# Output projections after two mixers: a weight tile's split is moved ahead, and one pair of output tiles goes k tile by k tile

## The chip, the core and the metric

The kernel runs on one core of a Trainium2 chip. The metric is the time of one execution on the device, in microseconds (us). Engines are named as in the profile: PE is TensorE (PEld its weight loads), DVE is VectorE, ACT is ScalarE, POOL is GpSimd, SP is SyncE, which here issues every DMA.

## What is computed

Two blocks of two layers each run one after the other. Each layer is a mixer and a convolutional FFN with residual sums and norms. Two mixers matter here, the "first" and the "second" one:

```python
def _even_mixer(h, w_in, w_out, lb, norm_g, sinks, cos, sin):      # first block, layer 0: the first mixer
    z = h @ w_in
    ...
    oa = _hgrn2(...)                       # 4 heads of 128
    oa = oa * rsqrt(mean(oa * oa) + eps) * norm_g
    oa = oa * silu(ag)
    ob = _swa(q, k, v, sinks)              # window attention, 8 heads of 64
    return jnp.concatenate([oa, ob], axis=-1) @ w_out          # "out1"

# second block, layer 0: the second mixer (even_mix), on 256 context and 512 latent tokens
#   fourier_mix: 4 groups of 128 columns;  gated linear attention: 4 heads of 128
#   each head: o * rsqrt(mean(o * o) + eps) * g_gla_out * silu(gate)
#   concatenate([fourier, gla]) @ w_even_out                   # "out2"
```

The modulation of every layer is `silu(c) @ w + b`, from the conditioning vectors c (three rows of 1024 in all). For the layers behind the first one these products are made on DVE during the FFNs.

## The kernel before, in words

**Layout.** Activations are kept transposed: a tile is 128 features by all tokens (512 latent tokens, or 768 with the 256 context tokens, which come as segments of 256 and 512 columns). A product is made at higher precision out of two fp32r parts: the activations lie in `h_hi` and `h_lo`, a weight tile in `w_hi` and `w_lo`, and each k tile (128 of the 1024 input features) takes three matmuls, hi by hi, lo by hi, and hi by lo, per segment. With 512 tokens an output tile is 8 k tiles x 3 = 24 matmuls, with 768 tokens it is 48.

**Weights.** All weight tiles of the program have one running number g. Tile g uses buffer g % 2 of `w_raw`, `w_hi`, `w_lo` and PSUM banks 2(g % 2) and 2(g % 2) + 1. Four steps belong to each tile, each on another engine and in that engine's own program order: `sp_fetch(g)` (L257, after `w_lo` of g - 2), `act_split(g)` (L267: ACT copies `w_raw` into `w_hi`, after the load and after the product of g - 2), `dve_split(g)` (L277: `w_lo` = `w_raw` - `w_hi`), `pe_product(g)` (L286). `pe_product` waits for `w_lo` of its tile and can wait for each k tile of the activations before its matmuls. `pe_pair` (L306) makes two output tiles together: k tile c of the first, then k tile c - 3 of the second. It is used at present for the first two tiles of the input projections and of the FFNs.

**Output projections.** `pe_residual`, `act_residual` and `dve_residual` (L1108 to L1150) run eight output tiles: tiles 22 to 29 for out1, 175 to 182 for out2. ACT's and DVE's loops split tile base + n + 1 at the head of step n, so the first tile (22, 175) is split at the end of the stage before and the second (23, 176) is the first thing of these loops. For out1, PE makes behind its second tile a small product, the "guess" of the mean (L1070), which waits for the first residual sum (`dve_add`, L340).

**Around out1.** ACT's order is: `act_window` (its last work is the four copies into `h_hi`, L944), `act_vectors` (L430: it waits for the DMA of all conditioning vectors into `c_act`, issued by SP in `sp_vectors` when the window attention's last product is done, and then applies SiLU to 128 x 3072), `act_tables` (a table load, L252), then `act_residual`. DVE's order is `dve_window` (ends with the four `h_lo`, L971), five small coefficient operations (L1214 to L1219), `dve_residual`. SP's is `sp_vectors`, three loads of `m_raw`, then `sp_tiles`, the first of which is tile 25's fetch, waiting for `w_lo` of tile 23.

**Around out2.** The last part of the second mixer, `pe_gla`, `act_gla` and `dve_gla`, goes head by head, 0 to 3, with PSUM banks 4 and 5 or 6 and 7: PE mixes (L1834 to L1836), ACT copies out and squares (L1873, L1879), PE sums the squares (L1840), ACT takes the root (L1884, L1887), DVE scales and gates (L1947, L1949), ACT makes `h_hi` (L500) and DVE `h_lo` (L506) of k tile 4 + h. k tiles 0 to 3 come from the Fourier part and are there long before. Then PE's `pe_out2` waits for `h_lo` of k tile 7, the last head's, ahead of its first matmul:

```python
def pe_out2(k):
    pe_residual(k, BASE["out2"], TALL, k.h_hi, k.h_lo, [("h_lo", ("gla", KD - 1))], ("rms", 1))
```

Of the kernel before, what the change touches and what calls it, by code (L numbers as in the profile page):

```python
# [17 lines left out]
KD = D // P  # L18
CTX, LAT = 256, 512
TALL = CTX + LAT  # L20
# [1084 lines left out]
        sp_fetch(k, base + i + 3)  # L1105


def pe_residual(k, base, tokens, hi, lo, ready, st):  # L1108

    for n in range(KD):  # L1110
        pe_product(k, base + n, tokens, hi, lo, ready if n == 0 else ())
        if n == 1 and st[0] == "ln":
            pe_guess(k, st, base)
    pe_sums(k, st)


def act_residual(k, base, st, split=None):

    for n in range(KD):
        act_split(k, base + n + 1)  # L1120
        if n == 2:
            if st[0] == "ln":
                act_guess(k, st)
            act_square(k, st, 0, base)
        if n >= 2:
            act_square(k, st, n - 1, base)
    if split is not None and st[0] == "ln":
        act_split(k, split)
    act_square(k, st, KD - 1, base)
    if split is not None and st[0] == "rms":  # L1130
        act_split(k, split)


def dve_residual(k, base, tokens, gates, st, slots=None, x_ready=None):
    for n in range(KD + 1):
        if n == 1 and x_ready:
            k.nc.vector.wait_ge(*k.seen(*x_ready))
        if n:
            dve_add(k, base + n - 1, n - 1, tokens, gates(n - 1))
        if n <= 2:  # L1140
            dve_split(k, base + n + 1)
        for f in (0, 1) if n == 2 else (n - 1,) if n > 2 else ():
            dve_center(k, st, f, base)
            dve_sum_x(k, st, f)
        if 2 < n < KD:
            dve_split(k, base + n + 1)
        for f in (0, 1) if n == 2 else (n - 1,) if n > 2 else ():
            dve_sum_squares(k, st, f)
        for j in slots[n] if slots and n < KD else ():
            dve_job(k, FFN_JOBS, j)  # L1150
# [692 lines left out]
def act_gla(k):  # L1843
    act = k.nc.scalar
    q, kk, (e0, e1), comb, _, turned, state = gl_views(k)
    v3 = lambda a: a.rearrange("p (n c) -> p n c", c=CHUNK)
    s16 = 1.0 / 16.0
    act_gl_gates(k, 0)
    for i in range(len(GL_STEPS)):
        act_decay(k, "g", i, gl_combs(k)[i % 3], s16)  # L1850
        if i == 2:
            act_gl_gates(k, 1)
    act.activation(k.gb_flat(4, 4), k.gb_flat(4, 4), ACT.Silu).then_inc(*k.tick("gl_silu"))
    act_tables(k)
    act.wait_ge(*k.seen("kd_arg", "g"))
    act.activation(comb, comb, ACT.Exp, scale=s16).then_inc(*k.tick("kd_decay", ("g", 0)))
    for d in range(2):
        for b in range(0, 12, 8):
            n = min(8, 12 - b)
            act.wait_ge(*k.seen("turn", ("gkd", d, b)))  # L1860
            got = k.ps[:, 4 + b // 4:6 + b // 4, :].rearrange("p b (i t) -> p (b i) t", t=P)[:, 0:n, :]
            act.activation(k.gkdt[d][:, b:b + n, :], got, ACT.Copy).then_inc(*k.tick("turned_out", ("gkd", d, b)))
        if d == 0:
            act.activation(comb, e1, ACT.Exp, scale=s16).then_inc(*k.tick("kd_decay", ("g", 1)))
    act.activation(e0, e0, ACT.Exp, scale=s16).then_inc(*k.tick("q_decay", ("g", 0)))
    act.wait_ge(*k.seen("q_arg"))
    act.activation(e1, e1, ACT.Exp, scale=s16).then_inc(*k.tick("q_decay", ("g", 1)))
    act.activation(k.gends[:, :, :], k.gends[:, :, :], ACT.Exp, scale=s16).then_inc(*k.tick("end_decay", "g"))
    for h in range(4):
        o, b0 = comb[:, (h % 2) * TALL:(h % 2 + 1) * TALL], 4 + 2 * (h % 2)  # L1870
        act.wait_ge(*k.seen("mixed", ("g", h)))
        for t0, tn, bank in segments(TALL):
            last = act.activation(o[:, t0:t0 + tn], k.ps[:, b0 + bank, 0:tn], ACT.Copy)  # L1873
        last.then_inc(*k.tick("mixed_out", ("g", h)))
        act.wait_ge(*k.seen("mixed_out", ("g", h)))
        for i, (t0, tn, bank) in enumerate(segments(TALL)):
            if h:
                act.wait_ge(*k.seen("summed", ("g", h - 1, i)))
            act.activation(k.tmp[i][:, 0:tn], o[:, t0:t0 + tn], ACT.Square).then_inc(*k.tick("squared", ("g", h, i)))  # L1879
        act.wait_ge(*k.seen("summed", ("g", h, 1)))  # L1880
        if h:
            act.wait_ge(*k.seen("normed", ("g", h - 1)))
        for t0, tn, bank in segments(TALL):
            last = act.activation(k.rstd[:, t0:t0 + tn], k.ps[:, b0 + bank, 0:tn], ACT.Ln, scale=1.0 / P, bias=k.col("eps6"))  # L1884
        last.then_inc(*k.tick("root_log", ("g", h)))
        act.wait_ge(*k.seen("root_log", ("g", h)))
        act.activation(k.rstd[:, :], k.rstd[:, :], ACT.Exp, scale=-0.5).then_inc(*k.tick("root", ("g", h)))  # L1887
        act_high(k, "gla", 4 + h, slice(0, TALL), o)


def dve_gla(k):
# [42 lines left out]
    for n in range(NC2 - 1):  # L1934
        for d in range(2):
# [6 lines left out]
                                                k.gends[:, d, f * NC2 + c:f * NC2 + c + 1], k.ps[:, bank, f * P:(f + 1) * P], ALU.mult, ALU.add)  # L1942
            last.then_inc(*k.tick("state", ("g", d, n + 1)))
    for h in range(4):
        o = comb[:, (h % 2) * TALL:(h % 2 + 1) * TALL]
        dve.wait_ge(*k.seen("root", ("g", h)))
        dve.scalar_tensor_tensor(o, o, k.col("ggla", h), k.rstd[:, :], ALU.mult, ALU.mult).then_inc(*k.tick("normed", ("g", h)))  # L1947
        dve.wait_ge(*k.seen("normed", ("g", h)))
        dve.tensor_tensor(o, o, k.z2[:, 4 + h, :], ALU.mult).then_inc(*k.tick("value", ("gla", 4 + h)))  # L1949
        dve_low(k, "gla", 4 + h, slice(0, TALL), o)  # L1950


def pe_out2(k):
    pe_residual(k, BASE["out2"], TALL, k.h_hi, k.h_lo, [("h_lo", ("gla", KD - 1))], ("rms", 1))

# [299 lines left out]
def act_program(k):  # L2257
    act_start(k)
    act_in1(k)
    act_hgrn(k)  # L2260
    act_window(k)
    act_vectors(k)
    act_tables(k)
    act_residual(k, BASE["out1"], ("ln", 0), BASE["up", 0, 0, 0] + 1)
    act_norm(k, 0, split=BASE["up", 0, 0, 0] + 1)
    act_ffn(k, 0, 0, LAT, ("ln", 1))
    act_norm(k, 1, plain=k.ph)
    act_residual(k, BASE["pool"], ("ln", 2), BASE["up", 0, 1, 0] + 1)
    act_norm(k, 2, split=BASE["up", 0, 1, 0] + 1)
    act_ffn(k, 0, 1, LAT, ("ln", 3), None, act_context)  # L2270
    act_norm(k, 3)
    act_rms(k, 0, LAT, BASE["in2"] + 1)
    act_in2(k)
    act_fourier(k)
    act_gla(k)
    act_residual(k, BASE["out2"], ("rms", 1), BASE["up", 1, 0, 0] + 1)
    act_rms(k, 1, TALL, BASE["up", 1, 0, 0] + 1)
    act_ffn(k, 1, 0, TALL, ("rms", 2), BASE["qkv"] + 1)
    act_rms(k, 2, TALL, BASE["qkv"] + 1)
    act_attention(k)  # L2280
    act_residual(k, BASE["attout"], ("rms", 3), BASE["up", 1, 1, 0] + 1)
    act_rms(k, 3, LAT, BASE["up", 1, 1, 0] + 1)
    act_ffn(k, 1, 1, LAT, ("rms", 4))
    act_final(k)


def dve_program(k):
    dve_start(k)
    dve_in1(k)
    dve_hgrn(k)  # L2290
    dve_window(k)
    dve_out1(k)
    dve_norm(k, 0, split=BASE["up", 0, 0, 0] + 1)
    k.nc.vector.wait_ge(*k.seen("c_act", "all"))
    dve_ffn(k, 0, 0, LAT, gates1(k, 0, 5), ("x_scaled", (0, KD - 1)), ("ln", 1), lambda: dve_coefficients1(k, 1, 0, 1, (0, 1, NMOD - 1)))
    dve_norm(k, 1, behind=lambda f: dve_pool_window(k, f))
    dve_pool(k)
    dve_norm(k, 2, split=BASE["up", 0, 1, 0] + 1)
    dve_ffn(k, 0, 1, LAT, gates1(k, 1, 5), ("x_scaled", (2, KD - 1)), ("ln", 3), lambda: dve_coefficients2(k, 0, 0, 0, "gmix", (1,)), dve_context)
    dve_norm(k, 3)  # L2300
    dve_rms(k, 0, LAT, BASE["in2"] + 1)
    dve_in2(k)
    dve_fourier(k)
    dve_gla(k)
    dve_coefficients2(k, 1, 0, 3, "gffn")
    dve_residual(k, BASE["out2"], TALL, gates2(k, 0, 2), ("rms", 1))
    dve_rms(k, 1, TALL, BASE["up", 1, 0, 0] + 1)
    dve_ffn(k, 1, 0, TALL, gates2(k, 0, 5), None, ("rms", 2), lambda: dve_coefficients2(k, 2, 1, 0, "gmix"))
    dve_rms(k, 2, TALL, BASE["qkv"] + 1)
    dve_attention(k)  # L2310
    dve_coefficients2(k, 3, 1, 3, "gffn", (1,))
    dve_residual(k, BASE["attout"], LAT, gates2(k, 1, 2), ("rms", 3))
    dve_rms(k, 3, LAT, BASE["up", 1, 1, 0] + 1)
    dve_ffn(k, 1, 1, LAT, gates2(k, 1, 5), None, ("rms", 4), lambda: None)
    dve_final(k)
# [133 lines left out]
```

## Time and profile before

| What | Value |
|---|---|
| Time, median of 3 runs | 3154.01 us (3152.72 to 3155.38) |
| Profiled execution: its own time / its span | 3153.78 us / 3152.5 us |
| PE busy | 2678.3 us (85%) |
| DVE busy | 1786.4 us (57%) |
| ACT busy | 1064.7 us (34%) |
| L301 (`pe_product`), three groups of 2464 matmuls | 818.4, 814.9, 814.6 us |
| L324 (`pe_pair`), hi by hi group, 144 matmuls | 58.6 us |
| Idle ahead of the L301 hi by hi group | 68.3 us, of it 38.6 us until DVE's `w_lo` |

How to read it: "busy" is the time in which an engine had an instruction running. A row of a timeline gives the start, the duration, the engine, the source line, what is written from what and how many instructions are merged; in brackets stands the idle time before it and what ended it. PE's granted clock is given as a share of full speed: 0.50 is 1.2 GHz and 1.00 is 2.4 GHz. PE rows overlap (each shows more than its own share of the array), so that the distance between starts says what a matmul costs.

### The profile page before, as it was taken

To read this page: it belongs to the slowest core of one execution; us is meant where nothing else is said; L and a number is where in the kernel's file an instruction comes from. 1 tells how busy PE (TensorE), PEld (TensorE's weight loads), DVE (VectorE), ACT (ScalarE), POOL (GpSimd) and SP (SyncE) were. 2 spreads that over 40 slices of the span, in tenths; PEclk is the share of its full clock that TensorE was granted. 3 is DMA by queue.
4 is the path that set the end of the run, shared out by engine and by line. 5 is a ranking of instruction groups with operands and counts; after the bars stand their busy time and mean duration, and the time that the engine had idled before them with its cause. 6 is when DMAs were issued, how large, how long until landed. Compare 5 with 4: busy or idle time off the path is not lost.

```text
span 3152.5 us, 31335 instructions
## 1 busy us (share of the span) xinstructions
PE 2678.3 (85%) x12792; PEld 2161.1 (69%) x12792; DVE 1786.4 (57%) x2396; ACT 1064.7 (34%) x1371; POOL 20.9 (1%) x31
## 2 busy tenths in 40 slices
PE   5945589999479999897656889999998966889998
PEld 4844468888358888685455678888886633578886
DVE  6575568887788877510494255525544155365464
ACT  3242343233353243422222243313323322254242
POOL 0000000000100000000000000000000000000000
PEclk9967789999779999998765899999998989999999
DMA  8600128755125665111000111211221100123232
GB/s 310 227 20 2 40 82 270 268 182 169 36 93 185 198 206 188 43 64 56 18 1 1 34 53 62 71 57 62 66 74 55 54 1 0 40 81 106 88 104 84
DMA packets 80270, 295.48 MB, mean 94 GB/s; under 512 B 8944, under 2 KB 11632, under 8 KB 79872
## 3 DMA queue, kind: packets, MB, share of 16 engines
q1 hardware_dynamic: 80128, 293.49, 27.9%
q8 instruction: 101, 1.65, 0.2%
q14 instruction: 41, 0.34, 0.0%
HBM read 291.35 MB, written 2.10 MB: 93 GB/s over the span
## 4 chain that ended last, share of the span: by engine, by line
PE 76%; DVE 14%; ACT 6%; issue 2%; DMA 0%; POOL 0%; SPq 0%; DVEq 0%; ACTq 0%
PE ps L301 64%; PE ps L2032 2%; PE ps L324 2%; PE ps L1661 1%; DVE gatt L665 1%; PE ps L654 1%; DVE anm L2159 1%; ACT h_hi L500 1%; ACT ascores L2111 1%; DVE h_lo L506 1%; ACT sq L1513 1%; DVE w_lo L282 1%; DVE hatt L665 1%; DVE aprobs L2134 1%; PE ps L909 1%
## 5 line engine op out<-in xcount | busy, mean ns | idle before, releaser
L301 PE MATMUL ps<-h_hi,w_hi 128*128 128x512 f32 (+1 forms) x2464 | 818.4, 369 | 68.3 <-DVE w_lo L282 38.6
L301 PE MATMUL ps<-h_hi,w_lo 128*128 128x512 f32 (+1 forms) x2464 | 814.9, 367 | 0.0
L301 PE MATMUL ps<-h_lo,w_hi 128*128 128x512 f32 (+1 forms) x2464 | 814.6, 367 | 0.0
L282 DVE TENSOR_TENSOR w_lo<-w_raw,w_hi 128x1024 fp32r<-128x1024 f32 (+2 forms) x323 | 414.8, 1284 | 616.3 <-ACT w_hi L274 615.6
L274 ACT ACTIVATE w_hi<-w_raw 128x1024 fp32r<-128x1024 f32 (+2 forms) x323 | 357.8, 1108 | 936.7 <-PE ps L301 914.9
L301 PEld LDWEIGHTS ps<-h_hi,w_hi 128*128 128x128 f32 x2464 | 465.8, 189 | 154.4 <-DVE w_lo L282 42.1
L301 PEld LDWEIGHTS ps<-h_hi,w_lo 128*128 128x128 f32 x2464 | 466.0, 189 | 77.4
L301 PEld LDWEIGHTS ps<-h_lo,w_hi 128*128 128x128 f32 x2464 | 466.1, 189 | 76.6 <-issue 0.7
L301 PE MATMUL ps<-g_hi,w_hi 128*128 128x512 f32 (+1 forms) x880 | 295.7, 369 | 0.8 <-DVE w_lo L282 0.8
L301 PE MATMUL ps<-g_hi,w_lo 128*128 128x512 f32 (+1 forms) x880 | 294.9, 368 | 0.0
L301 PE MATMUL ps<-g_lo,w_hi 128*128 128x512 f32 (+1 forms) x880 | 294.8, 368 | 0.0
L420 DVE CUSTOM_DVE_ANT_0 m_raw<-m_raw,c_act,small 128x1024 f32<-128x1024 f32 x179 | 226.7, 1281 | 1.4 <-DMA m_raw<-in_ada_w 1.3
L345 DVE SCALAR_TENSOR_TENSOR x<-ps,mods,x 128x512 f32<-128x512 f32 (+1 forms) x112 | 75.3, 691 | 212.3 <-PE ps L301 212.3
L301 PEld LDWEIGHTS ps<-g_hi,w_hi 128*128 128x128 f32 x880 | 165.3, 188 | 29.7 <-DVE w_lo L282 1.4
L301 PEld LDWEIGHTS ps<-g_lo,w_hi 128*128 128x128 f32 x880 | 165.3, 188 | 28.1 <-issue 0.5
L301 PEld LDWEIGHTS ps<-g_hi,w_lo 128*128 128x128 f32 x880 | 165.3, 188 | 27.8
L1380 DVE SCALAR_TENSOR_TENSOR conv_u<-ps,small,conv_u 128x510 f32<-128x510 f32 (+2 forms) x220 | 148.7, 693 | 3.1
L1336 ACT ACTIVATE g_hi<-gated 128x512 fp32r<-128x512 f32 (+1 forms) x88 | 60.5, 688 | 224.0 <-DVE gated L1393 224.0
L1331 ACT ACTIVATE silu_u<-conv_u 128x512 f32<-128x512 f32 (+1 forms) x88 | 60.6, 688 | 191.9 <-DVE conv_u L1380 191.9
L324 PE MATMUL ps<-h_hi,w_hi 128*128 128x512 f32 (+1 forms) x144 | 58.6, 444 | 73.4 <-DVE h_lo L506 38.8
L1395 DVE TENSOR_TENSOR g_lo<-gated,g_hi 128x512 fp32r<-128x512 f32 (+1 forms) x88 | 66.8, 759 | 66.3 <-ACT g_hi L1336 66.3
L324 PEld LDWEIGHTS ps<-h_hi,w_hi 128*128 128x128 f32 x144 | 30.4, 217 | 97.0 <-issue 73.9
(356 smaller groups left out, 2637.6 us busy)
## 6 DMA issues: line engine op xcount, KB each, us to landing
w_raw<-in_up SPq DMA_DIRECT2D x176, 512.0 KB, 3.3
m_raw<-in_w_mod SPq DMA_DIRECT2D x96, 512.0 KB, 3.3
w_raw<-in_down SPq DMA_DIRECT2D x64, 704.0 KB, 4.2
m_raw<-in_ada_w SPq DMA_DIRECT2D x83, 512.0 KB, 4.7
w_raw<-in_in SPq DMA_DIRECT2D x39, 512.0 KB, 3.3
w_raw<-in_out SPq DMA_DIRECT2D x16, 512.0 KB, 3.2
m_start<-in_ada_w SPq DMA_DIRECT2D x13, 512.0 KB, 11.6
w_raw<-in_qkv SPq DMA_DIRECT2D x12, 512.0 KB, 3.2
```

The source lines that it names most:

```text
L274: act.activation(k.w_hi[s][:, 0:w], k.w_raw[s][:, 0:w], ACT.Copy).then_inc(*k.tick("w_hi", g))
L282: dve.tensor_tensor(k.w_lo[s][:, 0:w], k.w_raw[s][:, 0:w], k.w_hi[s][:, 0:w].bitcast(F32), ALU.subtract).then_inc(*k.tick("w_lo", g))
L301: last = pe.matmul(ps[:, bank, 0:tn], a[:, c, :], b[:, c, t0:t0 + tn], start=c == 0 and n == 0, stop=c == kt - 1 and n == 2)
L324: last = pe.matmul(ps[:, bank, 0:tn], a, b[:, c, t0:t0 + tn], start=c == 0 and n == 0, stop=c == KD - 1 and n == 2)
L345: last = dve.scalar_tensor_tensor(x, k.ps[:, 2 * s + bank, 0:tn], gates[bank], x, ALU.mult, ALU.add)
L420: dve.tensor_tensor_reduce(w, w, k.c_act[:, last, :], 1.0, bias, ALU.mult, ALU.add, column(last)).then_inc(*k.tick("mods", job.key))
L665: dve.copy_predicated(att[:, b:b + 8, :], mask.unsqueeze(1).to_broadcast([P, 8, P]), got).then_inc(*k.tick("att", (label, i, b)))
L1331: act.activation(f["silu"][:, :], f["conv"][0][:, :], ACT.Silu).then_inc(*k.tick("silu", g))
L1336: act.activation(f["hi"][:, j, :], f["g"][:, :], ACT.Copy).then_inc(*k.tick("g_hi", (block, layer, half, j)))
L1380: last = dve.scalar_tensor_tensor(o, ps[:, bank, lo - d:hi - d], w, o, ALU.mult, ALU.add)
L1395: dve.tensor_tensor(f["lo"][:, j, :], f["g"][:, :], f["hi"][:, j, :].bitcast(F32), ALU.subtract).then_inc(*k.tick("g_lo", key))
L2032: last = pe.matmul(k.ps[:, 6 + sl, :], k.av[:, j, (h // 4) * P:(h // 4 + 1) * P], k.aprobs[:, j, :], start=j == 0, stop=j == NS - 1)
```

## The change

Out1: `act_split` of tile 23 stands directly behind `act_window`, ahead of `act_vectors`, and is left out of `act_residual`; DVE's order stays. Out2: `act_split` and `dve_split` of tile 176 stand at the head of step 3 of the head loops of `act_gla` and `dve_gla` and are left out of the residual loops; PE makes tiles 175 and 176 with `pe_pair`, which waits for each k tile's own `h_lo` instead of for the last one at the start. Nothing is computed otherwise or left out.

```diff
--- before.py
+++ after.py
@@ -1105,19 +1105,22 @@
         sp_fetch(k, base + i + 3)
 
 
-def pe_residual(k, base, tokens, hi, lo, ready, st):
-
-    for n in range(KD):
+def pe_residual(k, base, tokens, hi, lo, ready, st, paired=False):
+
+    if paired:
+        pe_pair(k, base, tokens, hi, lo, ready)
+    for n in range(2 if paired else 0, KD):
         pe_product(k, base + n, tokens, hi, lo, ready if n == 0 else ())
         if n == 1 and st[0] == "ln":
             pe_guess(k, st, base)
     pe_sums(k, st)
 
 
-def act_residual(k, base, st, split=None):
+def act_residual(k, base, st, split=None, ahead=0):
 
     for n in range(KD):
-        act_split(k, base + n + 1)
+        if n >= ahead:
+            act_split(k, base + n + 1)
         if n == 2:
             if st[0] == "ln":
                 act_guess(k, st)
@@ -1131,13 +1134,13 @@
         act_split(k, split)
 
 
-def dve_residual(k, base, tokens, gates, st, slots=None, x_ready=None):
+def dve_residual(k, base, tokens, gates, st, slots=None, x_ready=None, ahead=0):
     for n in range(KD + 1):
         if n == 1 and x_ready:
             k.nc.vector.wait_ge(*k.seen(*x_ready))
         if n:
             dve_add(k, base + n - 1, n - 1, tokens, gates(n - 1))
-        if n <= 2:
+        if ahead <= n <= 2:
             dve_split(k, base + n + 1)
         for f in (0, 1) if n == 2 else (n - 1,) if n > 2 else ():
             dve_center(k, st, f, base)
@@ -1867,6 +1870,8 @@
     act.activation(e1, e1, ACT.Exp, scale=s16).then_inc(*k.tick("q_decay", ("g", 1)))
     act.activation(k.gends[:, :, :], k.gends[:, :, :], ACT.Exp, scale=s16).then_inc(*k.tick("end_decay", "g"))
     for h in range(4):
+        if h == 3:
+            act_split(k, BASE["out2"] + 1)
         o, b0 = comb[:, (h % 2) * TALL:(h % 2 + 1) * TALL], 4 + 2 * (h % 2)
         act.wait_ge(*k.seen("mixed", ("g", h)))
         for t0, tn, bank in segments(TALL):
@@ -1942,6 +1947,8 @@
                                                 k.gends[:, d, f * NC2 + c:f * NC2 + c + 1], k.ps[:, bank, f * P:(f + 1) * P], ALU.mult, ALU.add)
             last.then_inc(*k.tick("state", ("g", d, n + 1)))
     for h in range(4):
+        if h == 3:
+            dve_split(k, BASE["out2"] + 1)
         o = comb[:, (h % 2) * TALL:(h % 2 + 1) * TALL]
         dve.wait_ge(*k.seen("root", ("g", h)))
         dve.scalar_tensor_tensor(o, o, k.col("ggla", h), k.rstd[:, :], ALU.mult, ALU.mult).then_inc(*k.tick("normed", ("g", h)))
@@ -1951,7 +1958,8 @@
 
 
 def pe_out2(k):
-    pe_residual(k, BASE["out2"], TALL, k.h_hi, k.h_lo, [("h_lo", ("gla", KD - 1))], ("rms", 1))
+    ready = [("h_lo", ("fourier", c)) for c in range(4)] + [("h_lo", ("gla", c)) for c in range(4, KD)]
+    pe_residual(k, BASE["out2"], TALL, k.h_hi, k.h_lo, ready, ("rms", 1), paired=True)
 
 
 
@@ -2259,9 +2267,10 @@
     act_in1(k)
     act_hgrn(k)
     act_window(k)
+    act_split(k, BASE["out1"] + 1)
     act_vectors(k)
     act_tables(k)
-    act_residual(k, BASE["out1"], ("ln", 0), BASE["up", 0, 0, 0] + 1)
+    act_residual(k, BASE["out1"], ("ln", 0), BASE["up", 0, 0, 0] + 1, ahead=1)
     act_norm(k, 0, split=BASE["up", 0, 0, 0] + 1)
     act_ffn(k, 0, 0, LAT, ("ln", 1))
     act_norm(k, 1, plain=k.ph)
@@ -2273,7 +2282,7 @@
     act_in2(k)
     act_fourier(k)
     act_gla(k)
-    act_residual(k, BASE["out2"], ("rms", 1), BASE["up", 1, 0, 0] + 1)
+    act_residual(k, BASE["out2"], ("rms", 1), BASE["up", 1, 0, 0] + 1, ahead=1)
     act_rms(k, 1, TALL, BASE["up", 1, 0, 0] + 1)
     act_ffn(k, 1, 0, TALL, ("rms", 2), BASE["qkv"] + 1)
     act_rms(k, 2, TALL, BASE["qkv"] + 1)
@@ -2303,7 +2312,7 @@
     dve_fourier(k)
     dve_gla(k)
     dve_coefficients2(k, 1, 0, 3, "gffn")
-    dve_residual(k, BASE["out2"], TALL, gates2(k, 0, 2), ("rms", 1))
+    dve_residual(k, BASE["out2"], TALL, gates2(k, 0, 2), ("rms", 1), ahead=1)
     dve_rms(k, 1, TALL, BASE["up", 1, 0, 0] + 1)
     dve_ffn(k, 1, 0, TALL, gates2(k, 0, 5), None, ("rms", 2), lambda: dve_coefficients2(k, 2, 1, 0, "gmix"))
     dve_rms(k, 2, TALL, BASE["qkv"] + 1)
```

## Rows read from the trace of the kernel before

**Rows 1.** The page: the chain that ended last, shares of the span by engine

```profile
PE 76%; DVE 14%; ACT 6%; issue 2%; DMA 0%; POOL 0%; SPq 0%; DVEq 0%; ACTq 0%
```

**Rows 2.** Chain of waits, 360 to 430 us: start us, us, what

```profile
382.48 6.62 DMA c_act<-in_c_rows
...
391.90 1.28 ACT L252
...
393.19 1.07 ACT w_hi L274
...
394.29 1.24 DVE w_lo L282
...
395.56 7.37 PE ps L301 x24
402.94 0.86 PE ps L1070 x2
```

**Rows 3.** Timeline, 368 to 425 us: start us, us, engine, line, operation, idle before

```profile
383.14 0.50 PE L301 MATMUL ps<-h_hi,w_hi 128*128 128x512 f32 x1 [0.69 <-ACT z L938]
...
383.47 0.40 PE L301 MATMUL ps<-h_lo,w_hi 128*128 128x512 f32 x1
...
385.33 1.28 ACT L432 ACT_TABLE_LOAD   x1
...
386.50 0.16 DVE L1219 TENSOR_TENSOR coef<-coef,mods 128x8 f32<-128x8 f32 x1
...
388.48 0.39 PE L301 MATMUL ps<-h_hi,w_lo 128*128 128x512 f32 x1
389.12 2.76 ACT L432 ACTIVATE c_act<-c_act 128x3072 f32<-128x3072 f32 x1 [2.50 <-DMA c_act<-in_c_rows]
...
403.87 0.40 PE L301 MATMUL ps<-h_lo,w_hi 128*128 128x512 f32 x1
```

**Rows 4.** PE by stretch, same stage: us, PE busy, granted clock, DMA share, GB/s

```profile
392.00:393.00 1.00, 0.00 (x0) 0.64 0.09 33
...
399.00:400.00 1.00, 1.00 (x5) 0.95 0.88 315
```

**Rows 5.** DMA issues, 380 to 410 us: count, KB each, median us to landing

```profile
m_raw<-in_ada_w SPq DMA_DIRECT2D x3, 512.0 KB, 8.3
w_raw<-in_out SPq DMA_DIRECT2D x3, 512.0 KB, 3.2
```

**Rows 6.** Timeline, 1715 to 1806 us

```profile
1754.69 0.84 ACT L500 ACTIVATE h_hi<-gcomb 128x768 fp32r<-128x768 f32 x1 [2.08 <-DVE gcomb L1949]
...
1756.95 0.87 ACT L1873 ACTIVATE gcomb<-ps 128x256 f32<-128x256 f32 x2 [1.42 <-PE ps L1836]
...
1758.32 2.93 PE L1840 MATMUL ps<-tmp,ones 128*128 128x256 f32 x4 [1.41 <-ACT tmp L1879]
...
1763.25 1.02 DVE L1947 SCALAR_TENSOR_TENSOR gcomb<-gcomb,small,rstd 128x768 f32<-128x768 f32 x1 [6.73 <-ACT rstd L1887]
...
1766.17 0.96 DVE L506 TENSOR_TENSOR h_lo<-gcomb,h_hi 128x768 fp32r<-128x768 f32 x1 [0.91 <-ACT h_hi L500]
...
1767.28 0.98 PE L301 MATMUL ps<-h_hi,w_hi 128*128 128x256 f32 x2 [6.03 <-DVE h_lo L506]
...
1768.06 0.84 PE L301 MATMUL ps<-h_lo,w_hi 128*128 128x256 f32 x2
...
1768.70 0.84 PE L301 MATMUL ps<-h_hi,w_lo 128*128 128x256 f32 x2
```

**Rows 7.** PE by stretch, the same stage

```profile
1771.00:1772.00 1.00, 1.00 (x7) 0.87 0.26 102
```

**Rows 8.** DVE timeline, 1776 to 1836 us

```profile
1777.82 1.14 DVE L345 SCALAR_TENSOR_TENSOR x<-ps,mods,x 128x256 f32<-128x256 f32 x2 [9.25 <-PE ps L301]
...
1786.30 1.14 DVE L345 SCALAR_TENSOR_TENSOR x<-ps,mods,x 128x256 f32<-128x256 f32 x2 [6.10 <-PE ps L301]
```

**Rows 9.** PE by stretch, the four heads' mixing

```profile
1730.00:1732.00 2.00, 2.00 (x8) 0.50 0.04 8
```

## Prediction

> **What bounds the kernel now.** I read the page's chain first: PE carries 76% of the chain that ended last [rows 1], so a gap of PE that nothing else covers goes into the time in full, and an edit on ACT or DVE counts only if PE starts something earlier for it. The chain of waits around out1 then leaves PE and goes through a DMA: `c_act` lands at 389.10 us, ACT's SiLU and a table load end at 393.18, only then come `w_hi` and `w_lo` of tile 23, and PE starts that tile at 395.56 [rows 2]. PE's last matmul of tile 22 is at 388.48 [rows 3]: it stands still for 6.7 us for a weight split that needs none of the vectors. Around out2, PE's last work of head 3, the sums of squares, ends at 1761.25 (1758.32 + 2.93), and tile 175 starts at 1767.28 after 6.03 us of idle time that end with the last head's `h_lo` [rows 6]. Seven of the eight k tiles were there all that time. Both gaps have a second price: after each of them the granted clock is 0.50, until 399.05 (the stretch from 399 shows 0.95) and until 1771.26 (the one from 1771 shows 0.87) [rows 4, 7].
>
> **Part A, tile 23's split ahead of the SiLU.** ACT is done with the `h_hi` copies at 385.33, where now a table load of 1.28 us stands [rows 3]. The split takes that place: 385.33 + 1.07 = 386.40. The table load then ends at 387.7, still ahead of the vectors at 389.10, so the SiLU begins when it did; what hides the split is the 2.50 us wait for that DMA [rows 2, 3]. DVE's coefficients end at 386.66 [rows 3]; its split follows until 386.7 + 1.24 = 387.94, ahead of PE's end of tile 22 (388.71) by 0.7 us. Tile 23 then runs without a gap.
>
> What is late next is tile 24. Its `act_split` stands behind SiLU and table load and takes over exactly tile 23's old times: `w_hi` from 393.19, `w_lo` until 395.53, PE at 395.56 [rows 2]. PE meanwhile does tile 23 at full clock: 24 matmuls at the spacing of tile 22, (388.48 - 383.47) / 22 = 0.228 us [rows 3], so 388.7 to 394.2, and the guess of 0.86 [rows 2] until 395.0. A gap of 0.5 us stays. With the first two matmul starts 0.33 apart, as after a short gap at full clock (383.14, 383.47), tile 24's second matmul starts at 395.89, where before it started at 403.87 [rows 3]. **Part A gives 8.0 us**: 6.7 of gap and some 1.8 of half clock and restart, less the 0.5 left.
>
> SP's queue moves as well: tile 25's fetch waits for `w_lo` of tile 23 and is issued at 388.0 instead of 395.5, behind three `m_raw` loads that take 8.3 us to land where a load by itself takes 3.2 [rows 5]. DMA is quiet from 392.1 (0.09 busy in that stretch [rows 4]), so it lands between 392 and 395.4; ACT asks for it at 394.3, and PE wants the finished tile at 401.0. Cost nothing, hidden by tile 24's 5.5 us. It is issued 1.1 us before `c_act` lands; if it took all the bandwidth from then on, the chain and tile 24 would slip by at most those 1.1. At 0 to -1.1 I take 0, since a queue that holds three earlier loads is the nearest row. Bounds of part A: 6.9, and 8.2 for reading the starts 0.2 wrong.
>
> **Part B, the pair in out2.** ACT's split of tile 176 stands behind `h_hi` of head 2, which ends at 1755.53, and ahead of the wait for head 3's mixing, which ended at 1756.95 after 1.42 us of idle time [rows 6]. At 1.07 it is done by 1756.6 and delays nothing, with 0.35 to spare; without that cover it would put its 1.07 on head 3, and so on PE's sums behind it. DVE's split (1756.6 to 1757.9) lies in the 6.73 us before head 3's root [rows 6]. The raw tile was fetched in the input projection, so ACT waits for no DMA; SP sends tile 178's fetch some 10 us earlier, on an empty queue. At 0 to -1.07 I take 0.
>
> PE starts the pair behind its sums, at 1761.26. It does 7 k tiles of tile 175 and 4 of 176 before it needs the last head's `h_lo` (1766.17 + 0.96 = 1767.13 [rows 6]). One k tile is 1.06 us at full clock (8.48 for 8, from the distance of two residual sums [rows 8]) and 1.92 at half (three times the 0.64 between 1768.06 and 1768.70 [rows 6]); eleven need 11.7 us or more, and there are 5.9. The pair never waits.
>
> Before, both tiles' work ended at 1786.24, just ahead of the second residual sum [rows 8]. After, it is 1761.26 + 16 x 1.06 = 1778.2, plus what the half clock costs: (1 - 1.06 / 1.92) = 0.45 us for each microsecond at 0.50. Before, the clock rose 4.0 us after PE resumed at out2, and 3.5 us after it resumed at out1 [rows 4, 7]; PE's unbroken work now begins with the sums at 1758.32, which puts the rise at 1761.8 to 1762.3, or, counted from the pair itself, at 1764.8 to 1765.3. I take the nearer middle, 1763, so 0.8 us; ends 0.2 and 1.8. The pair ends at 1779.0. **Part B gives 7.2 us**, bounds 5.1 (half clock 1.8 and the split uncovered) and 7.8.
>
> The next wait was checked: tile 177's split needs the product of 175, and in the pair only four k tiles (4.2 us) lie behind it instead of eight. DVE's residual sum and split take 1.14 + 1.24 [rows 2, 8] and about 0.1 of signals, 2.5 us in all. PE does not wait.
>
> On the clock the Trainium skill (TensorE: Matmul & The Clock Gate, "What's actually happening") says that the throttled state is the default and that activity releases it. By this rule alone the pair would find a full clock almost at once behind 2.93 us of sums, and part B would be 8.0, the sum 16.0. This case's trace agrees only in part: in the heads' mixing PE was busy for 2.00 of 2.00 us and the clock stood at 0.50 [rows 9].
>
> **Sum:** 8.0 + 7.2 = 15.2 us off the profiled execution's own 3153.78 us (its span is 3152.5), 3138.6; it lies 0.23 under the median of 3154.01, so I forecast 3138.8. Behind both places all waits hang on work that moves along, so nothing that I see gives it back.
>
> **Rivals.**
> 1. *Part B gains little or nothing* (chance 0.06): ACT's split is late after all and sits before head 3's copy, the raw tile is not there, or the clock stays at 0.50 through most of the pair, 16 us x 0.45 = 7.2 given back. For it: rows 9. Against: with the same matmuls as the pair's the clock rose in 4.0 us. Time 3154.0 - 8.0 = 3146.0.
> 2. *Part A gains nothing* (0.04): what PE waits for is in the end the DMA chain, and the later split of tile 24, or the queue behind it, takes the place of tile 23's. The chain shows how it would look, but one tile and the guess, 6.3 us, now lie under it. Time 3146.8.
> 3. *The gains are given back later* (0.04): the FFN behind out1 or out2 is paced by its DMA loads or DVE's modulation products, and meets them at another point. Against: these loads are issued off DVE's progress, which moves too. 3147 to 3154.
> 4. *Slower* (0.03): the clock does not rise in out2. PE enters it at 0.50 without the idle stretch that preceded the rise before, and activity is no guarantee [rows 9]. Each tile at half clock costs 8 x (1.92 - 1.06) = 6.9 us more, so beyond 15.2 / 6.9 = 2.2 tiles it is slower than before; with all eight at half clock 3154.0 - 15.2 - 0.8 + 55 = 3193. The stretch of half clock in the mixing lasted long; with fp32r matmuls of this shape no row shows more than 4.0 us.
>
> **How the numbers follow.** The forecast has 0.83. The known bounds give 6.9 + 5.1 = 12.0 to 8.2 + 7.8 = 16.0 us, 3138.0 to 3142.0. The three runs of before lie 2.7 us apart, and both edits shift all later work against the clock's rises and falls, which I can't place: some 3 us either way. That makes 3135.0 to 3145.0, which holds 8 in 10; the half gains lie just outside. A measurement of this kernel tells 0.2% (6.3 us) from no change: the forecast and the half gains of 7 or 8 us are faster by more, most of rival 3 is within, two thirds of rival 4 are slower: 0.93, 0.05, 0.02.
>
> **What would show it.** Right: `w_lo` of tile 23 done near 388 and no PE gap at 388.9; a gap of about 0.5 us ahead of tile 24, still ended by `w_lo` behind SiLU; the clock at 1.00 from 384 to 410; tile 24 eight us earlier. In out2, L324 starts within 0.3 us of the sums' end, some 6 k tiles or fewer are done when the last `h_lo` lands, no PE wait for tile 177, head 3's chain as long as before, and L324's hi by hi group grows from 144 to 176 matmuls while L301's shrinks to 2432. Wrong: head 3's copy later than its mixing; a half clock beyond 5 us of the pair; or a wait in the FFNs that grows by what out1 and out2 lost.

## The result, and the profile after

| | Before | After |
|---|---|---|
| Median of 10 runs each | 3152.01 us (3146.6 to 3158.43) | 3133.88 us (3130.16 to 3148.95) |
| Profiled execution: time / span | 3153.78 / 3152.5 us | 3134.42 / 3133.1 us |
| PE busy | 2678.3 us | 2671.2 us |

The ratio on record, which is taken over all runs and not from the two medians, is 0.9946, 95% interval 0.9931 to 0.9960: 17.0 us faster, 12.6 to 21.7 (the medians lie 18.1 apart). The forecast was 15.2 us less and a time of 3138.8 between 3135.0 and 3145.0; the measured time lies 1.1 us below that range.

The page of the kernel after, the engine row and two groups (out<-in, count | busy, mean ns | idle before):

```profile
PE 2671.2 (85%) x12792; PEld 2149.4 (69%) x12792; DVE 1786.1 (57%) x2396; ACT 1063.0 (34%) x1371; POOL 21.6 (1%) x31
...
L301 PE MATMUL ps<-h_hi,w_hi 128*128 128x512 f32 (+1 forms) x2432 | 809.1, 369 | 57.6 <-DVE w_lo L282 32.8
...
L324 PE MATMUL ps<-h_hi,w_hi 128*128 128x512 f32 (+1 forms) x176 | 67.9, 432 | 74.9 <-DVE h_lo L506 39.4
```

L324 grew by 32 matmuls to 176, L301's group shrank to 2432, and its idle time fell from 68.3 to 57.6 us, of which the wait for `w_lo` gave 38.6 - 32.8 = 5.8.

**Out1.** The chain of waits of the kernel after, 360 to 430 us (start, us, what), against [rows 2]:

```profile
380.39 6.47 DMA c_act<-in_c_rows
...
389.68 1.28 ACT L252
...
390.97 1.07 ACT w_hi L274
...
392.06 1.24 DVE w_lo L282
...
393.34 32.95 PE ps L301 x144
```

The chain still goes through the vectors' DMA, SiLU and table load, but now into tile 24. The timeline of the same stretch, against [rows 3]:

```profile
383.13 1.05 ACT L274 ACTIVATE w_hi<-w_raw 128x1024 fp32r<-128x1024 f32 x1
...
384.49 1.22 DVE L282 TENSOR_TENSOR w_lo<-w_raw,w_hi 128x1024 fp32r<-128x1024 f32 x1
...
386.88 2.78 ACT L432 ACTIVATE c_act<-c_act 128x3072 f32<-128x3072 f32 x1 [1.41 <-DMA c_act<-in_c_rows]
...
392.07 1.02 PE L1070 MATMUL ps<-x,ones 128*128 128x512 f32 x2
...
393.34 0.50 PE L301 MATMUL ps<-h_hi,w_hi 128*128 128x512 f32 x1 [0.25 <-DVE w_lo L282]
...
393.68 0.40 PE L301 MATMUL ps<-h_lo,w_hi 128*128 128x512 f32 x1
```

Tile 23's `w_hi` and `w_lo` are made from 383.13 to 385.7, 1.2 us ahead of the SiLU's start. PE runs tile 23 without a break into the guess (392.07) and waits 0.25 us for tile 24. From the SiLU's start (389.12, now 386.88) to tile 24's second matmul (403.87, now 393.68) it was 14.75 us and is 6.80: 7.95 us less. The same from the SiLU to the first norm behind out1, whose first instruction the timelines of before and of after show:

```profile
439.94 0.60 ACT L1169 ACTIVATE rstd<-ps 128x512 f32<-128x512 f32 x1 [1.28 <-PE ps L1085]
```

```profile
429.73 0.60 ACT L1172 ACTIVATE rstd<-ps 128x512 f32<-128x512 f32 x1 [1.28 <-PE ps L1085]
```

439.94 - 389.12 = 50.82 us before and 429.73 - 386.88 = 42.85 after: 8.0 us, none of it lost on the way.

**Out2.** Timeline of the kernel after, against [rows 6, 8]:

```profile
1743.43 1.04 ACT L274 ACTIVATE w_hi<-w_raw 128x1024 fp32r<-128x1024 f32 x1
...
1744.50 1.23 DVE L282 TENSOR_TENSOR w_lo<-w_raw,w_hi 128x1024 fp32r<-128x1024 f32 x1
...
1746.21 2.93 PE L1843 MATMUL ps<-tmp,ones 128*128 128x256 f32 x4 [1.41 <-ACT tmp L1884]
...
1749.17 1.05 ACT L1889 ACTIVATE rstd<-ps,small 128x256 f32<-128x256 f32 x2 [2.50 <-PE ps L1843]
1749.57 0.84 PE L324 MATMUL ps<-h_lo,w_hi 128*128 128x256 f32 x2
...
1754.06 0.96 DVE L506 TENSOR_TENSOR h_lo<-gcomb,h_hi 128x768 fp32r<-128x768 f32 x1 [0.91 <-ACT h_hi L500]
...
1763.33 1.14 DVE L345 SCALAR_TENSOR_TENSOR x<-ps,mods,x 128x256 f32<-128x256 f32 x2 [8.00 <-PE ps L324]
...
1764.48 1.23 DVE L282 TENSOR_TENSOR w_lo<-w_raw,w_hi 128x1024 fp32r<-128x1024 f32 x1
...
1767.37 0.51 PE L301 MATMUL ps<-h_hi,w_hi 128*128 128x256 f32 x2
```

The split on ACT ends at 1744.5, ahead of head 3's mixing; DVE's at 1745.7. PE goes from its sums straight into the pair; when the last `h_lo` is done (1754.06 + 0.96) it is in the fifth of the eleven k tiles that come before the one that needs it. The residual sum of tile 175 comes at 1763.33, `w_lo` of tile 177 is ready at 1765.7, and PE takes tile 177 at 1767.37 without a wait. PE by stretch in the same place (us, busy, granted clock), against [rows 7]:

```profile
1751.00:1752.00 1.00, 1.00 (x5) 0.50 0.00 0
1752.00:1753.00 1.00, 1.00 (x7) 0.89 0.00 0
1753.00:1754.00 1.00, 1.00 (x8) 1.00 0.00 0
```

The stretch with 0.89 puts the clock's rise at 1752.2; the sums had ended at 1749.14, so half clock took 3.1 x 0.45 = 1.4 us of the pair.

Where the 19.4 us between the two profiled spans went: 8.0 at out1 and 6.6 at out2 (from head 3's root to the norm's root: 1841.49 - 1761.29 = 80.20 before, 1822.76 - 1749.17 = 73.59 after). The other 4.8 us lie where nothing was changed. 2.1 are there already when the vectors' DMA is issued (382.48 and 380.39), ahead of the first edited instruction. Another 1.3 lie in the first FFN, between the norm behind out1 and the next norm, whose first instructions are these:

```profile
823.91 0.60 ACT L1169 ACTIVATE rstd<-ps 128x512 f32<-128x512 f32 x1 [1.28 <-PE ps L1085]
```

```profile
812.42 0.60 ACT L1172 ACTIVATE rstd<-ps 128x512 f32<-128x512 f32 x1 [1.28 <-PE ps L1085]
```

823.91 - 439.94 = 383.97 us before, 812.42 - 429.73 = 382.69 after. These 4.8 us are what the experiments had to explain.

### The profile page after: what moved, and what is told of

Read it like the earlier page. It is cut to its first block, busy times and chain, and to the rows that moved or that the text cites. A ratio compares the mean times of both kernels' runs of the same rounds, so it can differ in the third digit from the quotient of the medians.

```text
span 3133.1 us, 31335 instructions
## 1 busy us (share of the span) xinstructions
PE 2671.2 (85%) x12792; PEld 2149.4 (69%) x12792; DVE 1786.1 (57%) x2396; ACT 1063.0 (34%) x1371; POOL 21.6 (1%) x31
## 4 chain that ended last, share of the span: by engine, by line
PE 76%; DVE 14%; ACT 6%; issue 2%; DMA 0%; POOL 0%; SPq 0%; DVEq 0%; ACTq 0%
PE ps L301 64%; PE ps L324 2%; PE ps L2040 2%; PE ps L1664 1%; DVE gatt L665 1%; PE ps L654 1%; DVE anm L2167 1%; ACT h_hi L500 1%; ACT ascores L2119 1%; DVE h_lo L506 1%; ACT sq L1516 1%; DVE w_lo L282 1%; DVE hatt L665 1%; DVE aprobs L2142 1%; DVE x L1240 0%
## 5 line engine op out<-in xcount | busy, mean ns | idle before, releaser
L301 PE MATMUL ps<-h_hi,w_hi 128*128 128x512 f32 (+1 forms) x2432 | 809.1, 369 | 57.6 <-DVE w_lo L282 32.8
L301 PE MATMUL ps<-h_lo,w_hi 128*128 128x512 f32 (+1 forms) x2432 | 806.5, 367 | 0.0
L301 PE MATMUL ps<-h_hi,w_lo 128*128 128x512 f32 (+1 forms) x2432 | 805.1, 367 | 0.0
L301 PEld LDWEIGHTS ps<-h_hi,w_hi 128*128 128x128 f32 x2432 | 458.4, 189 | 141.6 <-DVE w_lo L282 36.2
L301 PEld LDWEIGHTS ps<-h_hi,w_lo 128*128 128x128 f32 x2432 | 458.5, 189 | 78.3
L301 PEld LDWEIGHTS ps<-h_lo,w_hi 128*128 128x128 f32 x2432 | 458.6, 189 | 77.7 <-issue 0.8
L301 PE MATMUL ps<-g_hi,w_hi 128*128 128x512 f32 (+1 forms) x880 | 295.8, 369 | 0.8 <-DVE w_lo L282 0.8
L301 PE MATMUL ps<-g_lo,w_hi 128*128 128x512 f32 (+1 forms) x880 | 294.9, 368 | 0.0
L301 PE MATMUL ps<-g_hi,w_lo 128*128 128x512 f32 (+1 forms) x880 | 294.9, 368 | 0.0
L301 PEld LDWEIGHTS ps<-g_hi,w_hi 128*128 128x128 f32 x880 | 165.2, 188 | 30.0 <-DVE w_lo L282 1.4
L301 PEld LDWEIGHTS ps<-g_lo,w_hi 128*128 128x128 f32 x880 | 165.2, 188 | 28.5 <-issue 0.5
L301 PEld LDWEIGHTS ps<-g_hi,w_lo 128*128 128x128 f32 x880 | 165.2, 188 | 28.4
L324 PE MATMUL ps<-h_hi,w_hi 128*128 128x512 f32 (+1 forms) x176 | 67.9, 432 | 74.9 <-DVE h_lo L506 39.4
L324 PEld LDWEIGHTS ps<-h_hi,w_hi 128*128 128x128 f32 x176 | 36.7, 213 | 99.8 <-issue 74.3
## 6 DMA issues: line engine op xcount, KB each, us to landing
m_start<-in_ada_w SPq DMA_DIRECT2D x13, 512.0 KB, 11.7
```

The source lines that it names most:

```text
L301: last = pe.matmul(ps[:, bank, 0:tn], a[:, c, :], b[:, c, t0:t0 + tn], start=c == 0 and n == 0, stop=c == kt - 1 and n == 2)
L324: last = pe.matmul(ps[:, bank, 0:tn], a, b[:, c, t0:t0 + tn], start=c == 0 and n == 0, stop=c == KD - 1 and n == 2)
```

## The experiments

Theory 1: both edits give what their places show, about 15 us, and the rest is scatter between executions. Theory 2: the shifted work gains 2 to 4 us more elsewhere. In what follows two distances of each profile stand for the places: **D1** from the SiLU's start to the first norm behind out1, and **D2** from head 3's root to the norm's root behind out2.

**e1_unchanged**, no edit.

> The kernel before once more, under another name: 0 us. Theory 1 (both edits give what their two places in the trace show, about 8.1 + 6.6 = 14.7 us, and the rest of the 17 to 18 us measured is scatter between executions): its runs and those of the kernel before have medians up to 3 us apart. Theory 2 (the change gives 2 to 4 us more elsewhere, through work that meets the clock's rises at better points): medians within 1 us, so that 3 us are more than scatter.

Measured: 3152.20 us median of 11 (3148.57 to 3157.93), 3153.87 before in 21 runs (3144.26 to 3158.59); ratio 1.0003 (0.9993 to 1.0013). The medians of one and the same kernel are 1.7 us apart here, under the 3 of theory 1 and over the 1 of theory 2, and single executions up to 14; as the ratio puts the two only 1 us apart, this counts little for theory 1. D1 50.97, D2 78.50.

**e2_split23_only**, part A alone:

```diff
     act_window(k)
+    act_split(k, BASE["out1"] + 1)
     act_vectors(k)
...
-    act_residual(k, BASE["out1"], ("ln", 0), BASE["up", 0, 0, 0] + 1)
+    act_residual(k, BASE["out1"], ("ln", 0), BASE["up", 0, 0, 0] + 1, ahead=1)
```

> Part A alone: tile 23's split ahead of the SiLU, out2 as before. Theory 1: 8 us faster, the norm behind out1 (first L1169 row) 10.2 - 2.1 = 8.1 us nearer to the start of the vectors' DMA. Rival (the two gains depend on each other or come back later): under 5 us, or over 10.

Measured: 3142.31 us, ratio 0.9964 (0.9952 to 0.9977), 11.3 us faster. D1 42.86, so 8.0 us at the place, as expected; D2 78.82. Its SiLU began 3.4 us earlier than before's, ahead of the edit. The time lies over the 10 us from which on the expectation counts for the rival, and the place gives 8.0: some 3 us more than the place, without any part B.

**e3_pair_only**, part B alone: the kernel after with the lines of e2 taken back.

> Part B alone: splits of tile 176 ahead of head 3 and the pair, out1 as before. Theory 1: 6.6 us faster (5.5 to 7.8 by where the clock rises), and with part A it sums to the whole change. Theory 2: 9 us or more, the surplus of the whole change sits here or in the stages behind out2.

Measured: 3146.73 us, ratio 0.9976 (0.9966 to 0.9985), 7.6 us faster, inside theory 1's 5.5 to 7.8. D1 51.00, D2 72.19.

**e4_both_again**, the change once more.

> The whole change once more. Theory 1: 14 to 16 us faster, the sum of the two runs of its parts within 3 us. Theory 2: 17 to 18 again.

Measured: 3132.19 us, ratio 0.9939 (0.9925 to 0.9952), 19.2 us faster. The two parts sum to 18.9, so no dependence between them shows. But 19.2 us is over the 14 to 16 of theory 1, and over the 17 to 18 of theory 2 too. D1 42.85, D2 73.61.

**e5_waits_only**, part A, and in out2 nothing but the per-k-tile waits:

```diff
 def pe_out2(k):
-    pe_residual(k, BASE["out2"], TALL, k.h_hi, k.h_lo, [("h_lo", ("gla", KD - 1))], ("rms", 1))
+    ready = [("h_lo", ("fourier", c)) for c in range(4)] + [("h_lo", ("gla", c)) for c in range(4, KD)]
+    pe_residual(k, BASE["out2"], TALL, k.h_hi, k.h_lo, ready, ("rms", 1))
```

> Part A, and in out2 nothing but the waits: tile 175 waits for each k tile's own h_lo, no pair, and tile 176's splits stay in the residual loops. Theory 1 (what counts is that PE starts behind its sums; 7 k tiles of one output tile take 7.4 us or more, longer than the 5.9 us until the last h_lo): as fast as the whole change, from head 3's root to the norm's root 73 to 74 us as with the pair (78.5 to 80.2 before), tile 176 without a gap, as its w_lo is there 7.4 us after the sums and tile 175 takes 8.5 or more. Rival (the pair and the early split are needed): a gap ahead of k tile 7 or of tile 176, 2 to 6 us of the gain gone.

Measured: 3144.34 us median of 7 (3131.47 to 3152.93), ratio 0.9963 (0.9945 to 0.9981). The time fell short of theory 1, but the profiled execution is the fastest of the seven, 3131.47 us, and its timeline shows that out2 itself does not need the pair:

```profile
1746.73 2.93 PE L1841 MATMUL ps<-tmp,ones 128*128 128x256 f32 x4 [1.41 <-ACT tmp L1880]
...
1754.58 0.96 DVE L506 TENSOR_TENSOR h_lo<-gcomb,h_hi 128x768 fp32r<-128x768 f32 x1 [0.91 <-ACT h_hi L500]
...
1755.75 1.22 DVE L282 TENSOR_TENSOR w_lo<-w_raw,w_hi 128x1024 fp32r<-128x1024 f32 x1
...
1759.56 1.14 DVE L345 SCALAR_TENSOR_TENSOR x<-ps,mods,x 128x256 f32<-128x256 f32 x2 [2.60 <-PE ps L301]
...
1767.88 1.14 DVE L345 SCALAR_TENSOR_TENSOR x<-ps,mods,x 128x256 f32<-128x256 f32 x2 [5.95 <-PE ps L301]
```

Sums end at 1749.66, the last `h_lo` at 1755.54, tile 176's `w_lo` (made at its old place behind head 3) at 1756.97, and tile 175's product only at 1759.5, when its residual sum begins; PE waits for nothing. D2 is 72.20, the same as e3's 72.19 with the pair.

**e6_vectors_later**, the whole change with two splits ahead of the SiLU:

```diff
     act_split(k, BASE["out1"] + 1)
+    act_split(k, BASE["out1"] + 2)
     act_vectors(k)
...
-    act_residual(k, BASE["out1"], ("ln", 0), BASE["up", 0, 0, 0] + 1, ahead=1)
+    act_residual(k, BASE["out1"], ("ln", 0), BASE["up", 0, 0, 0] + 1, ahead=2)
```

> The whole change, with tile 24's split ahead of the vectors' SiLU as well. Theory 1 (the chain over the vectors' DMA still sets tile 24, by the gap of 0.4 us ahead of it): the gap goes, PE runs from 381.1 to the end of out1, SiLU starts 1 us or more later and nobody waits; from the product of tile 22 to the norm 0.4 to 0.6 us less, in the time not to be told from the whole change. Rival (the SiLU, now in the way of tile 25's split, makes tile 25 wait): a gap ahead of tile 25, 1 to 3 us slower than the whole change.

Measured: 3132.59 us (3125.77 to 3139.32), ratio 0.9935 (0.9921 to 0.9948), the lowest ratio of all, but not told apart from the change. Its chain of waits no longer holds the vectors' DMA:

```profile
379.61 11.17 PE ps L301 x48
390.78 0.86 PE ps L1070 x2
391.64 32.70 PE ps L301 x144
```

PE goes from tile 22 to the end of out1 (its last tiles stand in the 32.70 us) without a gap. From the DMA's issue (378.95) to the norm (427.78) it takes 48.8 us, 49.3 in the change (380.39 to 429.73): 0.5 us, as expected.

**e7_waits_vectors_later**, e5 and e6 together.

> Both simplifications: the waits alone in out2, and two splits ahead of the SiLU in out1. Theory 1: 17 to 18.5 us faster than before, equal to the whole change within its scatter.

Measured: 3143.51 us median of 9 (3129.20 to 3151.23), ratio 0.9963 (0.9949 to 0.9976), 11.7 us faster: less than expected. In its profiled execution (3145.44 us) D2 is 73.61, so out2 is fine, but the FFN behind it takes 573.8 us (from the norm's root for the 512 latent tokens to the next norm's first) where before and after take 563.4 and 563.6. PE is busy all the time at full clock in both; the stretches of 40 us of e5 and of e7, 80 us into this FFN, differ in the number of matmuls alone:

```profile
1903.60:1943.60 40.00, 40.00 (x232) 35.27 (x232) 21.23 (x30) 14.41 (x20) 0.00 (x0) 1.00 0.20 66
```

```profile
1905.40:1945.40 40.00, 40.00 (x228) 34.68 (x227) 21.79 (x31) 13.01 (x18) 0.00 (x0) 1.00 0.20 66
```

232 against 228 is 1.8%, and over 563 us that makes 9.9 of the 10.4 us. e3's profile, its slowest execution, had this pace there too (573.4 us); in the input projection of the second mixer 6 of the 18 profiles have it, with and without the change (e1, e3, e5, e9, e10 and the kernel after).

**e8_double_copy**, a second copy of the split's size at head 3:

```diff
             act_split(k, BASE["out2"] + 1)
+            act.activation(k.gkdt[0][:, 0:8, :].rearrange("p n c -> p (n c)"), k.gkdt[1][:, 0:8, :].rearrange("p n c -> p (n c)"), ACT.Copy)
```

> The whole change with a second ACT copy of 128x1024 (into a tile that is free by then) behind the split at head 3. Theory 1 (the split hides in the 1.42 us that ACT waits for head 3's mixing): two of them, 2 x 1.0 us, stick out, so that head 3's copy starts 0.5 to 0.8 us after its mixing's end instead of 0.3, and PE's sums and the pair come as much later. Rival (ACT has more room than the row shows): no shift.

```profile
1744.72 1.04 ACT L274 ACTIVATE w_hi<-w_raw 128x1024 fp32r<-128x1024 f32 x1
...
1745.67 1.04 ACT L1875 ACTIVATE gkdt<-gkdt 128x1024 f32<-128x1024 f32 x1
...
1746.62 0.85 ACT L1879 ACTIVATE gcomb<-ps 128x256 f32<-128x256 f32 x2
...
1747.97 2.93 PE L1843 MATMUL ps<-tmp,ones 128*128 128x256 f32 x4 [1.75 <-ACT tmp L1885]
```

Head 3's copy (1746.62) starts straight behind the second copy, and PE waits 1.75 us for the squares of head 3 where it waits 1.41 in the change: two copies stick out by 0.34 us. So the cover is real, and about as wide as the row of before said. Behind the end of its mixing it starts 0.40 us, where the expectation had 0.5 to 0.8; in the change it is 0.04. The time of its two executions was 3133.65 us (3130.26 and 3137.03).

After eight runs the change stood at 17 to 19 us, with 15 at its places. Two further theories were set against each other. Theory 3: the surplus is luck, since the clock in the last window mixing ahead of out1 and the matmul pace in stages with 768 tokens are drawn anew in each execution. Theory 4: the clock there depends on where tile 23's split stands.

**e9_unchanged_again**, no edit.

> The kernel before, a third profile. Seen so far: the last window mixing ahead of out1 (PE at 374 to 380) ran at half clock in the two profiles of it and at full clock in five of the six with the split of tile 23 moved; and the stages with 768 tokens run their matmuls at one of two paces, 117 to 118 or 115 in 20 us, through a whole stage. Theory 3 (both are drawn anew in each execution, and the surplus of 3 us over the 14.7 of the two places is such luck): 3152 to 3154 us, the clock there either way. Theory 4 (the half clock there belongs to the kernel before): half clock again, vectors' DMA issued at 382 to 383.

Measured: 3155.36 us median of 12 (3148.33 to 3162.93), ratio 1.0013 (1.0001 to 1.0026) against 3151.19 of the same kernel beside it: 4 us apart, with an interval that leaves 1 out, and no edit. Half clock again in the last window mixing, as theory 4 has it; D1 50.94, D2 80.19.

**e10_split23_again**, as e2.

> Part A alone again. Theory 3: between 8 and 11 us faster, with all its runs pooled nearer to 8 than the 11 of the first time. Theory 4: 11 again, vectors' DMA issued at 379.

Measured: 3140.37 us, ratio 0.9959 (0.9944 to 0.9973), 12.9 us: over the 8 to 11 of theory 3, and nearer to the 11 of theory 4. D1 42.89. D2, without the pair, 80.19. The vectors' DMA came as theory 4 had it, at 379.

**e11_waits_again**, as e5.

> Part A and the waits alone in out2, again. Before, four of seven executions took 3144 to 3153 and three 3131 to 3135, and its sister's profile at 3145 us showed the FFN behind out2 at the slow pace (115), 10.4 us longer, with out2 itself free of gaps. Theory 3 with this: again two groups, 10 to 15 us apart, and the profiled execution's pace in that FFN tells which group it is in (117 to 118: under 3137; 115: over 3141). Rival (the waits alone leave a stall that the first profile missed): no two groups, or a slow execution with the fast pace.

Measured: 3134.80 us median of 6 (3132.06 to 3139.66), ratio 0.9943 (0.9927 to 0.9959), one group only, as the rival had it, with the profile at the fast pace. The four times over 3144 us of e5 did not come back. D2 72.18.

**e12_both_third**, the change.

> The whole change, third time. Theory 3: 14 to 19 us faster, most executions in the fast group of that FFN, one in ten or so 10 us slower. Rival (pair and waits alone are alike and only luck parts them): as many slow executions as with the waits alone.

Measured: 3131.30 us (five from 3129.10 to 3133.20, one at 3147.91), ratio 0.9941 (0.9918 to 0.9964). D2 70.46.

**e13 to e16**, two single executions of the kernel before and two of part B alone, each with its profile.

> One look at the kernel before. Theory 3 (the clock in the last window mixing is drawn anew): full clock in one of two looks or so. Theory 4 (the place of tile 23's split decides it): half clock in all looks without that split moved, 0 of 4 so far at full, against 8 of 10 with it.

> One look at part B alone, which has out1 as before. Theory 3: full clock in the last window mixing in half of the looks. Theory 4: half clock.

> As e13: theory 3 full clock in half of the looks, theory 4 never.

> As e14: theory 3 full clock in half of the looks, theory 4 never.

Full clock in e13, e14 and e15, half in e16. With the four earlier profiles without the moved split that is 3 of 8; with it, 8 of 10. Two executions of one and the same kernel, before, in the last window mixing (us, PE busy, granted clock), first e9, then e13:

```profile
376.00:378.00 2.00, 0.57 (x3) 0.50 0.00 0
378.00:380.00 2.00, 2.00 (x11) 0.50 0.00 0
```

```profile
376.00:378.00 2.00, 2.00 (x24) 1.00 0.00 0
378.00:380.00 2.00, 1.31 (x11) 1.00 0.13 43
```

Theory 4 falls as it was put: the clock of this stretch differs between executions of one kernel, it costs or saves about 3 us, and e13 and e15 (3145.75 and 3146.56 us) are faster than before's profile by 7 to 8 us with no edit at all.

**The places, over all profiles** (e6 and e7 have no D1, as their SiLU is moved). Out2 runs at one of two paces: its output tiles stand 8.48 us apart in some profiles ([rows 8], and the kernel after) and 8.32 in others (e1, e3), with and without the change, so that D2 is compared at one pace:

| | without | with | gain |
|---|---|---|---|
| D1, tile 23's split (8 profiles without, 8 with) | 50.63 to 52.07, mean 51.0 | 42.85 to 42.89, mean 42.9 | 8.1 us |
| D2, pair, tiles 8.48 us apart (4 without, 3 with) | 80.19 to 80.20 | 73.49 to 73.61 | 6.6 us |
| D2, pair, tiles 8.32 us apart (3 without, 5 with) | 78.50 to 78.82 | 72.18 to 72.20, once 70.46 | 6.4 us |
| D2, waits alone (e5 and e11 at 8.32, e7 at 8.48) | | 72.20, 72.18; 73.61 | 6.4; 6.6 us |

**Where part A's other microseconds are.** The first FFN, from the norm behind out1 to the next norm, takes 383.9 to 384.9 us in seven of the eight profiles without tile 23's split moved, and 382.1 to 382.7 in all ten with it, e2 (part A alone) among them. From the SiLU to that next norm it is 434.5 to 435.9 us without (8 profiles) and 425.0 to 425.5 with (8): 10.1 us, of which D1 holds 8.1. PE by stretch (us, PE busy, granted clock), counted from the norm behind out1; first before:

```profile
439.90:443.90 4.00, 1.43 (x3) 0.52 0.00 0
...
448.00:457.00 9.00, 8.31 (x17) 0.50 0.09 37
...
439.90:479.90 40.00, 28.72 (x90) 0.70 0.31 105
```

the kernel after:

```profile
429.70:433.70 4.00, 0.85 (x2) 1.00 0.00 0
...
429.70:469.70 40.00, 28.07 (x95) 0.79 0.33 107
```

then e2 and e15:

```profile
428.60:468.60 40.00, 29.14 (x97) 0.79 0.33 114
```

```profile
437.30:477.30 40.00, 28.06 (x95) 0.79 0.35 107
```

Before, the clock falls at the norm and stands at half for 24 of the next 40 us; after, it falls some 5 us later and stands at half for 17. This goes with when the clock falls and not with the moved instruction itself: e15 is the kernel before, its clock too falls 5 us behind the norm, and its FFN takes 382.7 us (its D1 is the 52.07 of the table, so that its sum, 434.8, is that of the other seven). That the removed gap and half clock in out1 are what moves the later fall is argued from these profiles, not shown by an edit.

## Why the prediction was right or wrong

**What was right.** Tile 23's part of the working came as written: `w_lo` came long ahead of PE, the SiLU kept its time, tile 24's splits took over tile 23's old distance to the DMA, the clock stayed at full from tile 22 through out1, and a gap remained ahead of tile 24, 0.25 us instead of 0.5. At its place part A was put at 8.0 us and shows 8.0 to 8.1. Part B was put at 7.2 and shows 6.6, at the pace of before; the half clock of the pair, put at 0.8 us with ends 0.2 and 1.8, was 1.4 in the profile after. ACT's split was hidden, as e8 shows with its price, and tile 177 did not wait. By the rule of the Trainium skill (TensorE: Matmul & The Clock Gate, "What's actually happening"), that activity releases the throttle, part B would have been 8.0; the clock rose 3.1 us behind the sums and not at once, so the 7.2 by the rows was the nearer one.

**What failed, first: part A's sum ends at tile 24.** It prices the gap and the half clock behind it, and takes it that all later work moves along unchanged; that this work meets the clock's falls elsewhere was put at nothing in the sum and stands only in the range, as "some 3 us either way". The runs show a gain there: 1.9 us in the first FFN, some 1.5 of them in its opening, where the half clock was 7 us shorter. Part A is 10.1 us from the SiLU to the second norm, over its upper bound of 8.2. The row was to be had in the trace of before: rival 4 says that with fp32r matmuls of this shape no row shows more than 4.0 us of half clock, but behind the norm PE is busy with matmuls of 128x512 for 8.31 of 9.00 us at 0.50 (448 to 457). This is theory 2 of the experiments, with 1.9 us where it had 2 to 4.

**Second, the step "how the numbers follow".** It took the three runs of before, 2.7 us apart, for the scatter, added 3 us either way, and hung the absolute time on their median, 3154.01. In the sets of several runs the unchanged kernel took 3142.97 to 3162.93 us in 87 executions (mean 3153.1), with medians from 3151.19 to 3155.36 from set to set; the ten beside the result had 3152.01, 2.0 us lower than the three. Part A 2.1 us larger, part B 0.6 smaller and this 2.0 turn 3138.8 into 3135.3, the very edge of the range, and the 1.4 us from there to 3133.88 are within the scatter. So the range was too narrow for a single set, and which side of its edge the time fell on is luck. What differs between executions of one kernel are three things of some 2 to 10 us: the clock in the last window mixing (3 us), the matmul pace in stages with 768 tokens (2 to 3 us in the input projection, about 1.5 in out2, 10.4 in the FFN), and the clock among the heads (up to 4 us from one head to the next, as e1's and e13's profiles show against before's).

**What stays open.** Pooled over the sets of several runs the whole change is 18.8 us faster (21 executions, mean 3134.4), part A alone 12.3 (12 executions, 3140.8) and part B alone 6.8 (11, 3146.3). Part B agrees with its 6.4 to 6.6. Of part A's 12.3, 10.1 lie between the SiLU and the second norm, and some 1.5 ahead of it: the ten profiles with the moved split reach the vectors' DMA 2.8 us earlier than before's on average, the eight without 1.3. Whether this part would go away with more executions, or whether the moved instruction has some way to favour the full clock in the window mixing (8 of 10 profiles with it, 3 of 8 without), 18 profiles do not settle. Nor is it settled whether the waits alone are as good as the pair. In out2 they are. But in the set of e5 to e8, 10 of the 16 executions with the waits alone (e5, e7) took over 3140 us and none of the 8 with the pair (e6, e8); in the other sets it was none of 6 (e11) against 2 of 21 with the whole change. e7's profile has the slow pace in the FFN behind out2; whether the unprofiled ones over 3140 us had it, and whether the waits bring it, no run shows.

**The rivals.** None came: no part lost its gain, nothing was given back, and the clock rose in the pair. "Part B gains little" was closest in one point, the half clock at the pair's start, which took 1.4 us where 0.8 was forecast.

## What to carry to other kernels

Ask of every wait in the chain whether the work behind it needs what is waited for: here a weight split stood behind a DMA of vectors on ACT's queue for 6.7 us that PE paid, plus the half clock after the gap. If one output tile's k tiles are longer than the wait for the last of them, a wait per k tile closes the gap; the pair and its early split gave nothing on top at the place (at equal pace D2 72.2 against 72.2 and 73.6 against 73.6), though the total times leave it open. Judge an edit of 0.5% by the distance between two marks in several profiles, and set the second mark behind the next stage too: here the first FFN held 1.9 us of part A's 10.1. Take the range of a forecast from more than three runs.

## What the runs showed of the hardware that was not expected

Back-to-back matmuls at full clock have two paces in the stages whose matmuls alternate between 256 and 512 columns: 232 to 233 in 40 us (e5) or 228 to 229 (e7), 8.32 or 8.48 us for an output tile, held from a stage's start to its end. One stage's pace does not fix the next one's: e1 has the slow one in the input projection and the fast one in out2 and the FFN, e7 the fast one in the input projection and the slow one in both others. The stages of 512 columns only show 89 to 90 in every 20 us (before, after and e9). PE was busy for the whole of both. What decides it was not found.
